# Router of a two-layer encoder trunk: fewer filler products on TensorE, one copy moved to ScalarE, ranks in two products

## The reference

```python
def moe_ffn(h, w_router, b_router, w_gate, w_up, w_down):
    hf = h.reshape(B * S, D)
    logits = (hf @ w_router).astype(jnp.float32) + b_router.astype(jnp.float32)
    top_v, top_i = lax.top_k(logits, TOP_K)
    top_w = jax.nn.softmax(top_v, axis=-1)
    combine = jnp.sum(jax.nn.one_hot(top_i, N_EXPERTS, dtype=jnp.float32) * top_w[..., None], axis=1)
    out = jnp.zeros_like(hf)
    for e in range(N_EXPERTS):
        out = out + combine[:, e:e + 1] * swiglu(hf, w_gate[e], w_up[e], w_down[e])
    return out.reshape(B, S, D)
```

## Time and profile before

| | |
|---|---|
| median of 3 runs | 1521.96 us (1521.42 to 1522.92) |
| span of the profiled execution | 1527.8 us |
| that execution's own time | not given apart from its span |
| TensorE busy | 1460.7 us, 96% |
| weight loads of TensorE | 1011.2 us, 66% |
| VectorE, ScalarE busy | 754.8 us (49%), 585.3 us (38%) |
| moved by DMA | 473.73 MB, mean 310 GB/s |
| chain that ended last | TensorE 77%, DMA 17%, VectorE 4% |

### The profile page before, as it was taken

How to read it: one execution, slowest core, us unless ns; L and a number is a source line. 1 busy time by engine, 2 the same in 40 slices (tenths; PEclk the granted TensorE clock), 3 DMA queues, 4 the chain that set the end, 5 groups by cost and what they waited for, 6 DMA issues and landing times.

```text
span 1527.8 us, 17749 instructions
## 1 busy us (share of the span) xinstructions
PE 1460.7 (96%) x7506; PEld 1011.2 (66%) x7506; DVE 754.8 (49%) x809; ACT 585.3 (38%) x621; POOL 13.3 (1%) x18
## 2 busy tenths in 40 slices
PE   8999999999999999999999899999988899999876
PEld 7988888888888988888343368873423588734223
DVE  7448686555557548674112059851010499610203
ACT  4357664443334447651000057740000477500001
POOL 1000010000000000010000000000000000000000
PEclk9999999999999999997999999999999999999998
DMA  8353265555554353286999999999999999999995
GB/s 349 110 221 124 97 248 196 190 192 185 183 183 166 111 221 124 97 341 273 427 430 429 430 429 430 430 420 430 429 431 429 430 429 431 408 431 429 430 429 229
DMA packets 42959, 473.73 MB, mean 310 GB/s; under 512 B 5392, under 2 KB 5520, under 8 KB 7424
## 3 DMA queue, kind: packets, MB, share of 16 engines
q1 hardware_dynamic: 42048, 467.97, 75.3%
q0 software_dynamic: 832, 4.63, 0.8%
HBM read 471.53 MB, written 1.05 MB: 309 GB/s over the span
## 4 chain that ended last, share of the span: by engine, by line
PE 77%; DMA 17%; DVE 4%; ACT 1%; issue 1%; SPq 0%; DVEq 0%; ACTq 0%
PE ps L1884 17%; PE ps L1885 17%; PE ps L1886 17%; PE ps L2303 12%; DMA raw_a<-in_w_item 11%; DMA raw_b<-in_w_item 6%; PE ps L2338 5%; PE ps L2260 1%; PE ps L1920 1%; PE ps L2083 1%; PE ps L2050 1%; PE ps L2310 1%; PE ps L1914 1%; PE ps L2073 1%; DVE lo_a L1601 1%
## 5 line engine op out<-in xcount | busy, mean ns | idle before, releaser
L1187 DVE TENSOR_TENSOR lo_a<-raw_a,w_hi 128x2048 fp32r<-128x2048 f32 (+1 forms) x109 | 240.2, 2211 | 126.3 <-ACT w_hi L809 125.7
L1884 PE MATMUL ps<-w_hi,act_hi 128*128 128x512 f32 (+1 forms) x640 | 246.8, 386 | 1.5 <-DVE act_lo L1292 1.5
L809 ACT ACTIVATE w_hi<-raw_a 128x2048 fp32r<-128x2048 f32 (+1 forms) x109 | 200.7, 1849 | 118.8 <-PE ps L1886 118.7
L1885 PE MATMUL ps<-lo_a,act_hi 128*128 128x512 f32 (+1 forms) x640 | 243.2, 380 | 0.0
L1886 PE MATMUL ps<-w_hi,act_lo 128*128 128x512 f32 (+1 forms) x640 | 242.9, 380 | 0.0
L2303 PE MATMUL ps<-raw_b,x_small 128*64 128x512 f32 (+1 forms) x784 | 151.1, 534 | 10.5 <-DMA raw_b<-in_w_item 10.5
L2303 PE MATMUL ps<-raw_a,x_small 128*64 128x512 f32 (+1 forms) x736 | 147.3, 548 | 10.9 <-DMA raw_a<-in_w_item 10.9
L1096 ACT ACTIVATE hidT<-ps 128x512 f32<-128x512 f32 (+1 forms) x24 | 13.1, 544 | 331.3 <-PE ps L2310 331.3
L1884 PEld LDWEIGHTS ps<-w_hi,act_hi 128*128 128x128 f32 x640 | 121.1, 189 | 25.6 <-issue 2.4
L1886 PEld LDWEIGHTS ps<-w_hi,act_lo 128*128 128x128 f32 x640 | 120.8, 189 | 23.2
L1885 PEld LDWEIGHTS ps<-lo_a,act_hi 128*128 128x128 f32 x640 | 121.0, 189 | 21.2
(11 more groups left out here) (287 smaller groups left out, 1933.3 us busy)
## 6 DMA issues: line engine op xcount, KB each, us to landing
raw_b<-in_w_item SPq DMA_DIRECT2D x84, 2048.0 KB, 23.3
raw_a<-in_w_item SPq DMA_DIRECT2D x82, 2048.0 KB, 23.7
raw_a<-in_w_mix SPq DMA_DIRECT2D x60, 1024.0 KB, 5.0
raw_a<-in_w_item SPq DMA_DIRECT2D x42, 1024.0 KB, 5.0
raw_a<-in_w_mix SPq DMA_DIRECT2D x8, 512.0 KB, 3.5
ln_gb<-in_ln_mix POOLq DMA_DIRECT2D x2, 1024.0 KB, 4.8
raw_x<-in_w_item SPq DMA_DIRECT2D x1, 2048.0 KB, 15.7
raw_b<-in_w_item SPq DMA_DIRECT2D x2, 1024.0 KB, 28.7
```

The lines of the kernel that those rows point to most:

```text
L809: nc.scalar.activation(w_upper(g)[:, 0:n], raw(slot)[:, 0:n], ACT.Copy).then_inc(s_hi, 1)
L1187: nc.vector.tensor_tensor(w_lo(slot)[:, 0:n], raw(slot)[:, 0:n], w_upper(g)[:, 0:n].bitcast(F32), ALU.subtract).then_inc(s_lo, 1)
L1884: nc.tensor.matmul(dst, xh, wh, start=start, stop=False)
L1885: nc.tensor.matmul(dst, xh, wl, start=False, stop=False)
```

## The change

Four identity products stand behind each tile's router products, and none ahead of the gather. ScalarE copies both halves of tile 0; VectorE copies only the right half of tile 1, so `s_rta` counts three copies and `s_rtv` one. The ranks of both tiles come from two products: the triangle times both tiles' `sel` (16 columns), and the block of ones times tile 0's `sel` added to tile 1's half. `s_rk` is signalled after these, the counts follow with a semaphore of their own, `s_cnt`, for which VectorE waits before it copies them.

```diff
             def router_copy(t):
-                act.wait_ge(s_tp, 28 + 2 * t + 1)
-                nc.scalar.activation(x_rt[:, 0:4, t * P:t * P + P], ps[:, LATE_JOB[2 * t][2], :].rearrange("p (k n) -> p k n", k=4),
-                                     ACT.Copy).then_inc(s_rta, 1)
+                for half in range(1 if t else 2):
+                    act.wait_ge(s_tp, 28 + 2 * t + half + 1)
+                    nc.scalar.activation(x_rt[:, 4 * half:4 * half + 4, t * P:t * P + P],
+                                         ps[:, LATE_JOB[2 * t + half][2], :].rearrange("p (k n) -> p k n", k=4),
+                                         ACT.Copy).then_inc(s_rta, 1)
...
                 def router_copy(step):
-                    if step % 2:
+                    if step == 3:
...
             gather_matrix(lambda t: rkm[:, t, FIRST_EXPERT:FIRST_EXPERT + 1], False)
+            dve.wait_ge(s_cnt, 1)
             link(nc.vector.tensor_copy(cnt, ps[:, 7, 0:N_EXP]))
...
                 turn_norm(3, t, LATE_JOB)
-                pe.wait_ge(s_rta, t + 1)
-                pe.wait_ge(s_rtv, t + 1)
+                pe.wait_ge(s_rta, 2 + t)
+                if t:
+                    pe.wait_ge(s_rtv, 1)
...
-                keep_warm((14, 8)[t], 2)
+                keep_warm(4, 2)
             pe.wait_ge(s_sel, 1)
-            nc.tensor.matmul(ps[:, 6, 0:N_EXP], tri[:, 0, 0:P], sel[:, 0, :], start=True, stop=True)
-            for k in range(TILES):
-                nc.tensor.matmul(ps[:, 6, N_EXP:2 * N_EXP], tri[:, k, P:2 * P], sel[:, k, :], start=(k == 0), stop=(k == TILES - 1))
+            both = ps[:, 6, 0:TILES * N_EXP]
+            nc.tensor.matmul(both, tri[:, 0, 0:P], sel.rearrange("p t e -> p (t e)"), start=True, stop=False)
+            nc.tensor.matmul(both[:, N_EXP:2 * N_EXP], tri[:, 0, P:2 * P], sel[:, 0, :], start=False, stop=True).then_inc(s_rk, 1)
             for k in range(TILES):
                 ins = nc.tensor.matmul(ps[:, 7, 0:N_EXP], tri[:, 0, P:2 * P], sel[:, k, :], start=(k == 0), stop=(k == TILES - 1))
-            ins.then_inc(s_rk, 1)
-            keep_warm(8, 2)
+            ins.then_inc(s_cnt, 1)
             gather(0, False, FIRST_BANKS)
```

More of the change, by code:

```diff
@@ L546, in build @@
         s_rk = sem("ranks_summed")
+        s_cnt = sem("tokens_counted")
         s_tab = sem("items_listed")
```

## The result

The changed kernel takes 1527.03 us (median of 20 runs, 1524.62 to 1528.52), the kernel before 1522.70 in the same comparison (20 runs, 1519.90 to 1526.93). The ratio is 1.0026, 95% interval 1.0019 to 1.0032: slower by some 4 us. The profiled execution of the changed kernel has a span of 1524.9 us and a time of its own of 1526.65, so 1.8 us lie around the span. Added to before's span of 1527.8 this makes 1529.6, dearer than each of the 20 runs of before: the trace of before showed an unfavourable execution, and against it the changed one looks 2.9 us faster, while it is slower against the typical one. Three executions among all those behind this document (1634.51, 1837.30 and 2978.12 us) lay far outside the rest and are left out of every ratio and range, though not of the medians.

What follows compares the result with a forecast made beforehand. Bound: the chain through item 0's first products, which restart the weight stream. Against the profile 2.35 us gained (1527.8 to 1525.4); against the median of 1521.96 a cost of 1.9, so 1523.9, said as 1524; range 1518 to 1527.

Steps and rivals of the forecast that it cites:

- the stretch at half rate: Start of item 0 at the lower clock for 3.4 to 5.8 us, a loss of 1.7 to 2.9, taken as 2.3.
- the sum: Router against the profiled execution: item 0 in effect at 717.55 instead of 719.90, 2.35 us gained, span 1527.8 to 1525.4.
- The price of the gather: The gather's 32 records at the lower clock, taken at 0.213 each like 8-column products: 6.8 us; bounds 3.6 to 6.8.
- Rival 4: Gather: clock up, or unneeded, so it ends at 712.1; gain 3.5 to 7.8 us, 1514 to 1518.5; chance 0.11.
- The two edits that save time of their own: Router: ScalarE's copy of tile 0 gains 0.6 us, and the ranks in two products, signalled before the counts, 1.3.
- rival 5: End of the kernel: the change does nothing there, as a transfer hides it: 1522 us; chance 0.08.
- the hole: Weight stream ahead of item 0: slots full, SyncE issues a pair at 704.06 and the next only 19.8 us later.
- against the median: Last step: kernel before typically has item 0 at 715.6, changed kernel near 717.5, so the change costs 1.9 us: 1523.9.
- the forecast's own range: Lower clock through router and gather, before's typical run at 715 to 717: +0.5 to +2.8 us, 1522.5 to 1524.8; chance 0.42.
- rival 2: Router: runs before had an early clock rise, item 0 at 712.9 to 714.1; +3.4 to +4.6, 1525.4 to 1526.6; chance 0.25.

Runs made afterwards that it cites:

- the pair of profiles above: The profiles of the changed kernel (1527.03 us) and of the kernel before with only its identity products changed to 4, 4, 0 (1527.83 us).
- 4, 4, 0: Kernel before with only its identity products changed: 4 behind tile 0, 4 behind tile 1, none ahead of the gather; 1527.83 us, ratio 1.0040.
- the best kernel: Changed kernel with 4 identity products ahead of each tile's router products, 14 and 10 behind them, 2 behind the counts; 1518.44 us, ratio 0.9974.
- 14, 4, 0: Changed kernel with 14 identity products put back behind tile 0, 4 behind tile 1, none ahead of the gather; 1525.95 us, ratio 1.0017.
- 4 + 14, 4 + 10, 2: Identity products ahead of + behind tile 0's, then tile 1's router products, then behind the counts; in the kernel before, only these changed: 1521.26 us, ratio 0.9978.

## Why the prediction was right, and where it was off

**The steps in the profile.** Counted from the first transposes (692.01 before, 691.04 after):

| step | predicted | after |
|---|---|---|
| router products of tile 0 | 2.0 | 1.8 |
| transposes of tile 1 | 6.7 | 6.8 |
| router products of tile 1 | 9.3 | 9.6 |
| ranks | 14.7 | 15.2 |
| gather | 16.4 | 17.0 |
| item 0 | 23.2 | 24.0 |
| item 0, had it run at full clock | 25.5 | 25.6 |

The last line adds half of the stretch at half rate, booked as 2.3 us and measured as 1.5 (715.1 to 718.2). Before, item 0 stood at 27.9, so the router is 2.3 us shorter than in before's profile, where the sum had 2.35; a further 1.0 us lies ahead of the router, and 2.9 of the two together reach the end of the span. That the totals agree to 0.1 us is luck in part: ranks and gather came 0.5 to 0.6 us later than booked and item 0 began 0.8 later, and the half-rate start cost 0.8 less.

**The price of the gather.** Booked by the row of the 8-column products, 6.8 us; measured 7.0, in each of the six profiles where the clock stayed down. The weight loads under it were recorded at a mean of 332 ns each at 0.50 (after the change) and 192 ns at 1.00 (four ahead of the router products). The Trainium skill's figure for a weight load (TensorE: Matmul & The Clock Gate, section on LDWEIGHTS), by which the gather was estimated to stay near 3.4 us at either clock, does not hold here: 32 records took 7.0 us at 0.50 and 3.7 at 1.00. Rival 4 fell too: the clock was down and the gather felt it.

**The two edits that save time of their own** do so where nothing hides it: 1.9 us for copy and ranks in the pair of profiles above, 1.9 booked. **Nothing hidden by the stream** (rival 5): the issue after the hole moved with item 0.

**The step that was mis-sized** is the last, "against the median". I set before's typical item 0 at 715.6, which takes off 4.3 us for the clock of before's profile, and so the cost at 1.9 to 2.0. Measured is 4.0 us (2.9 to 4.9 by the interval). Put on the median of 1521.96, the ratio gives 1525.9: outside the forecast's own range of 1522.5 to 1524.8, and inside rival 2's. The wider range, 1518 to 1527, holds that figure; the median of the comparison, 1527.03, lies 0.03 past its edge, so that range held by little. By the same sum, 717.55 less 4.0, before stands at 713.5: under the 714.5 that rival 2 named as the point from which it decides. So the mechanism was that of the forecast, and the size that of rival 2, to which I gave 0.25. I had left part of the 5.8 us between before's span and its median to the recording. The profile after has a time of 1526.65, close to its kernel's median, so recording costs nothing that can be seen, and with the 1.8 us around the span the profiled execution of before was some 6.9 us dearer than the median: by these sums about 6 in the router and 1.0 ahead of it. No typical execution of before was profiled; 713.5 is worked out and not seen.

**Is it the clock, and not the identity products' own time?** Fewer of them made the kernel slower (e.g. 4, 4, 0 in the kernel before: ratio 1.0040), none equals four, more made it faster (0.9974), and more of the same, but of 8 columns, slowest of all (1.0051). The runs of one program point the same way: 29 runs of the kernel before in one comparison go from 1520.65 us at a mean granted clock of 0.997 to 1528.80 at 0.990, and over all 29 the time falls as the clock rises (correlation -0.89). The changed kernel's median clock is 0.988, the best kernel's 0.996. The Trainium skill (the same page, Part 1) says that the moment of the rise shifts from run to run, by some 500 ns. This case agrees that it shifts, but by far more: in the profiles of before and of the old identity products with the new copy and ranks, whose identity products are the same, the clock rose at 716.4, as the gather began, and at 706.5, ahead of the ranks.

Not all of the spread is the router's. The first transposes start anywhere from 689.54 to 692.01 in the fourteen profiles, with the same code ahead of them. The two earliest (689.54, 689.67) had no fall of the clock up to 680 us, the latest two (691.68, 692.01) one each at the start, behind 120 and behind 580 us.

**Still open:** how the gain divides between the products ahead of the router products and those behind them. None, two and four ahead gave 0.9983, 0.9979 and 0.9974, all within each other's intervals. Their runs spread over 6.8, 5.2 and 2.8 us, but the first figure hangs on one run of twelve (2.2 without it), and the sets of the third, in the kernel before, spread over 5.7. Open too is why the clock falls in one execution and holds in another of the same code: up to the identity products of tile 0, changed kernel and 14, 4, 0 run the same, and in the one profile it fell at 694.3, in the other at 704.1.

## What to carry to other kernels

Filler work that holds TensorE's clock is judged by the clock of the stretch that follows, over many runs: here 44 of 60 identity records went, 9.7 us of TensorE's time at 0.22 each (an estimate), and the gather's start came 7.6 us earlier on paper. What they bought, a gather of 3.7 instead of 7.0 us, a full-rate start of item 0 and, by the medians, often an earlier rise of the clock than in the profile of before, was worth more. In this kernel such products paid where the engine waits anyway, 128 columns wide, and in sets of 14 and 10; sets of four showed no gain over none. And before a change is costed against a profile, ask where that one execution lies among the timed runs: when the kernel's time hangs on a clock that may or may not rise, one profile can show either end.

## What the runs showed of the hardware

- TensorE unbroken in both products and weight loads, but for 0.3 us, ran at a granted clock of 0.50 for 24 us when its products, but for the tiles' transposes, were 8 to 64 columns wide (the run with 8-column identity products); the same sequence with 128-column identity products ran at 1.00 from end to end in its profile.
- Float32 products with weight loads of 128 columns followed the clock: 0.22 us from one gather record to the next at 0.50, with loads recorded at 332 ns, and 0.116 at 1.00, with loads of 192 ns.
- One program, undisturbed, spread over 8 us (0.5%), its slower executions at the lower mean clock. The sets 4 + 14, 4 + 10, 2 had a spread of 2.8 us with the new copy and ranks and of 5.7 with the old ones.
